# 320 free bytes in front of the activation tiles of a one-core transformer kernel

## The reference: what is computed

```python
def swiglu(h, w_gu, w_down):
    gate, up = jnp.split(h @ w_gu, 2, axis=-1)
    return (jax.nn.silu(gate) * up) @ w_down

for layer in range(2):
    x = x + 0.5 * swiglu(rmsnorm(x, ffn1_norm[layer]), ffn1_w_gu[layer], ffn1_w_down[layer])
    x = x + mixer(rmsnorm(x, mix_norm[layer]))
    x = x + 0.5 * swiglu(rmsnorm(x, ffn2_norm[layer]), ffn2_w_gu[layer], ffn2_w_down[layer])
x = rmsnorm(x, final_norm)
proj = rms_norm(x) @ w_in                      # second block
x = x + (gates0 * (attn @ w_up_attn) + gates1 * (rw @ w_up_rwkv)) @ w_out
x = x + jnp.square(jax.nn.relu(rms_norm(x) @ w_ff1)) @ w_ff2
x = x + (p @ w_ple) * jax.nn.sigmoid(rms_norm(x) @ w_ple_gate)
```

## The kernel before, in words

| tiles | place before |
|---|---|
| `w_hi`, `raw`, `w_lo` (all slots), `xT`; also `q_dec` and `att_t` of group 1, `gram_raw`, `x_raw`, `xt_raw` | 128 |
| `p_hi`, `p_lo` | 64 |
| `sq`, `rstd`, `full3` | 832 |
| `h_hi`, `h_lo`, `g_hi`, `g_lo`, `act2`, `full2`, `qkv`, `ao_*`, `mg_*`, `rw_*`, `gram` | 832 |
| `ba_hi`, `ba_lo`, `o_hi`, `o_lo`, `state_a`, `v_new`, `q_dec` and `att_t` of group 0 | 576 |
| `x_r`, `xt_r` | 64 |

## Time and profile before

### The profile page before, as it was taken

The page is one execution under the profiler, slowest core; times in us unless marked ns, Lnnn a source line. Parts: engine busy times, 40 slices in busy tenths (PEclk is TensorE's granted clock), DMA queues, the critical chain, the costliest instruction groups (busy, mean ns, idle before and its releaser), DMA issues. The chain is left out here.

```text
span 1605.0 us, 36127 instructions
## 1 busy us (share of the span) xinstructions
PE 1536.2 (96%) x15669; PEld 1478.2 (92%) x15669; DVE 1064.6 (66%) x1277; ACT 730.3 (46%) x814; POOL 69.9 (4%) x52
## 2 busy tenths in 40 slices
PE   7999989999999999999998999999997889999998
PEld 6999989878999999999988999999886778999997
DVE  5766487764867547664677766467768776777436
ACT  5443345543534344433446433354565444555333
POOL 2000000100100001000101000021000000100000
PEclk9999999999999999999999999999999999999999
DMA  8665545201556556555533555564320012555552
GB/s 269 189 192 201 185 157 169 96 2 51 183 188 193 200 184 184 183 184 187 181 131 96 182 187 191 185 201 145 120 79 3 3 56 81 184 184 189 202 186 79
DMA packets 155065, 243.26 MB, mean 152 GB/s; under 512 B 9283, under 2 KB 106174, under 8 KB 154814
## 3 DMA queue, kind: packets, MB, share of 16 engines
q1 hardware_dynamic: 154510, 240.63, 45.7%
q10 hardware_dynamic: 432, 0.79, 0.2%
HBM read 240.34 MB, written 1.05 MB: 150 GB/s over the span
## 5 line engine op out<-in xcount | busy, mean ns | idle before, releaser
L2888 DVE TENSOR_TENSOR w_lo<-raw,w_hi 128x2048 fp32r<-128x2048 f32 x225 | 522.9, 2335 | 243.0 <-ACT w_hi L2715 242.1
L2518 PE MATMUL dense_ps<-h_hi,w_hi 128*128 128x256 f32 x2368 | 668.3, 282 | 12.2 <-DVE h_lo L2963 8.6
L2519 PE MATMUL dense_ps<-h_lo,w_hi 128*128 128x256 f32 x2368 | 662.0, 280 | 0.0
L2520 PE MATMUL dense_ps<-h_hi,w_lo 128*128 128x256 f32 x2368 | 662.0, 280 | 0.0
L2715 ACT ACTIVATE w_hi<-raw 128x2048 fp32r<-128x2048 f32 x225 | 428.5, 1913 | 332.6 <-DMA raw<-in_ffn_w_down 116.2
L2518 PEld LDWEIGHTS dense_ps<-h_hi,w_hi 128*128 128x128 f32 x2368 | 450.5, 190 | 18.3 <-issue 17.8
L2519 PEld LDWEIGHTS dense_ps<-h_lo,w_hi 128*128 128x128 f32 x2368 | 447.4, 189 | 0.8 <-issue 0.5
L2520 PEld LDWEIGHTS dense_ps<-h_hi,w_lo 128*128 128x128 f32 x2368 | 448.1, 189 | 0.0
L2520 PE MATMUL dense_ps<-g_hi,w_lo 128*128 128x256 f32 x960 | 266.9, 278 | 0.0
L2518 PE MATMUL dense_ps<-g_hi,w_hi 128*128 128x256 f32 x960 | 266.9, 278 | 0.0
L2519 PE MATMUL dense_ps<-g_lo,w_hi 128*128 128x256 f32 x960 | 266.9, 278 | 0.0
(11 more groups left out here) (554 smaller groups left out, 1750.5 us busy)
## 6 DMA issues: line engine op xcount, KB each, us to landing
raw<-in_ffn_w_gu SPq DMA_DIRECT2D x176, 512.0 KB, 4.6
raw<-in_ffn_w_down SPq DMA_DIRECT2D x88, 512.0 KB, 4.1
raw<-in_w_ff SPq DMA_DIRECT2D x64, 512.0 KB, 4.2
raw<-in_w_in SPq DMA_DIRECT2D x36, 512.0 KB, 4.4
raw<-in_a_w_in SPq DMA_DIRECT2D x32, 512.0 KB, 4.3
raw<-in_a_w_out SPq DMA_DIRECT2D x8, 512.0 KB, 4.0
raw<-in_b_w_in SPq DMA_DIRECT2D x8, 512.0 KB, 4.2
raw<-in_b_w_out SPq DMA_DIRECT2D x8, 512.0 KB, 4.1
```

Of the source, the lines that this page charges most:

```text
L2518: pe.matmul(o, hi, mh, start=start, stop=False)
L2519: pe.matmul(o, hi, ml, start=False, stop=False)
L2520: return pe.matmul(o, lo, mh, start=False, stop=stop)
L2888: dve.tensor_tensor(w_lo[:, p % SLOTS, :], raw[:, p % SLOTS, :], w_hi[:, p % SLOTS, :].bitcast(F32), ALU.subtract).then_inc(lo_ready, 1)
```

## The change

Behind `full3` and in front of `h_hi` 320 bytes of each partition are left free. Everything that is placed from `h_at` or `arena` on moves up by 320 bytes; `y_tok`, which is placed from the end of the memory, stays. No instruction is added, removed or moved in order; only the addresses of the tiles change.

```diff
@@ -213,6 +213,7 @@
     sq = fixed.take("sq", [P, KD, T])
     rstd = fixed.take("rstd", [P, T])
     full3 = fixed.take("full3", [P, 3, 2, T])
+    fixed.at += 320
     h_at = fixed.at
     h_hi = fixed.take("h_hi", [P, KD, T], F32R)
     h_lo = fixed.take("h_lo", [P, KD, T], F32R)
```

## The result

The changed kernel takes **1652.36 us**, the median of four executions (1650.19 to 1656.09). The kernel before took 1603.21 us beside it (four executions, 1600.39 to 1608.98). The ratio is 1.0304, with a 95% interval of 1.0267 to 1.0341: slower by 3%, 49.2 us. The forecast was 1601.8 us with a range up to 1630, so it was wrong; the time is that of the rival "an even distance costs" (1650 us).

A forecast was written before the change was run, and what follows sets the result against it. The prediction took the pace of TensorE's large matmuls to bound the kernel. All terms were 0, leaving the profiled 1607.0 us, or 1601.8 us by the median of the other executions; range 1580 to 1630 us.

The forecast's parts named there:

- an even distance costs: Slower rival, large matmuls at L2518 to L2520: even distances in 64-byte units pace at 119.6 ns, 1650 us; chance 0.10.
- Instructions, queues, waits: 0.: Whole kernel: no instruction or wait added, removed or moved, every queue issues the same DMAs; cost 0.
- VectorE and ScalarE: 0, within 0.3 us.: Tiles moving from 832 to 128 keep their instruction times; only L618 might change, by 0.3 us either way; taken as 0.
- Addresses of the large matmuls: TensorE's 10,800 large matmuls: the moved operand leaves their pace alone; taken as 0, bounds -91.0 to +48.3 us.
- (a): L723 reads `q_dec` at distance 0 or 64 from `state_a`: 111.5 ns per step either way, so place does nothing.
- (b): Both paces occur at distance 192, and at 448 as well, so the present distance does not choose the pace.
- (c): Gate logits, distance 256, have a third pace, 119.6 ns, but also one place in PSUM and stationary tiles at 576.
- All at 119.6: +48.3 us: Bound for the large matmuls: 6,077 fast ones lose 6.4 ns each and 4,723 slow ones 2.0 ns.
- Faster: place decides which pace is stable.: Rival: an equal place puts every restart of the large matmuls into the fast pace, -20.8 us, 1581.0 us; chance 0.14.
- The farther form: Faster rival extended: large matmuls lose all excess over their columns, 106.7 ns each, 1511 us; below 113.2 ns chance 0.05.
- The sum that the prediction has by this figure: Large matmuls all at the skill's 109.2 ns, if place alone keeps the kernel from it: -67 us.
- One pace rules in all five feed-forwards: Sign that the forecast is wrong; if right, ffn0, ffn1, ffn4 stay fast and ffn2, ffn3 slow.

The follow-up runs named there:

- the 14 to 5 groups at 704: Kernel without the computation, 20 groups of 48 float32r matmuls behind growing waits at distance 704: 14 at 113.3 ns, 5 at 117.8.
- the sweeps: Kernels without the computation, only groups of float32r matmuls with the distance of moving operand from weights varied: 113.3 ns at 112, 120.0 at 0.
- the version at 128: Against the kernel before: `h` and `g` each cut from one tile, data 32 bytes in, distance 128 from the weights; 1641.25 us, ratio 1.0189.

## Why the prediction was wrong, point by point

**Instructions, queues, waits: 0.** Right. The counts are the same on every engine, and TensorE's longest waits in the hybrid stage are on the same lines with the same lengths (5.5 us behind `bk`, in both).

**VectorE and ScalarE: 0, within 0.3 us.** Right. The pair of the earlier trace rows after the change (group on VectorE by shape, 1220 to 1400 us):

```profile
L619 DVE COPY_PREDICATED xt_raw<-msk,gram_raw 128x128 f32<-128x128 uint8 x4 | 2.3, 568 | 0.0
L619 DVE COPY_PREDICATED xt_r<-msk,gram 128x128 f32<-128x128 uint8 x4 | 1.9, 484 | 0.0
```

`gram` came to 128, the place of `gram_raw`, and the difference of 84 ns (76 before) stayed, so the place of `gram` was never its cause. `xt_r` (384) still lies elsewhere than `xt_raw` (128), so its place is not cleared.

**"Addresses of the large matmuls ... I take 0, being nearest to (a)".** This is the step that failed: the term put at 0 measured 4.5 ns on each of the 10,800 matmuls, 49 us. Of the three rows I weighed, I chose one that could not speak. (a) are float32 matmuls, and they take 111.5 ns at the distances 0, 64, now 256, and in the run with 384 free bytes 192 (modulo 256): this form has no such effect at these places, while float32r has 120.0 ns at 0 and 113.3 or 117.8 at 64 and 192. I had written down the difference in type and passed over it. (b) "So the present distance does not choose the pace" was true, and the 14 to 5 groups at 704 confirm that a restart has a part in it. But it says only that this distance has two paces; that another has one of its own was left possible, and I read it as excluded. (c) was the right row: the only float32r matmuls of 256 columns at an even distance, with the only third pace. I discounted it for its one place in PSUM and its stationary tiles at 576. Both were innocent: the large matmuls have the same 120.0 ns without either, and the gate logits themselves have 113.3 ns once only their distance changes. Among three rows, the one with the same type and shape should have carried the term.

**The size of the rival.** "All at 119.6: +48.3 us" against a measured 49.2. The pace is 120.0 and not 119.6 (+4.3 us over 10,800; the 119.6 was 120.0 read from rounded starts), the mean of before 115.4 and not 115.1 (-3.2, in part because the counts of the earlier trace rows took in two or three matmuls too many, so that 113.3 and 117.8 came out as 113.2 and 117.6). That the two mis-sizes nearly cancel is luck. The rule named with it (in units of 64 bytes, even is slow and odd is not) held in every sweep of this form with the weights and the moving tiles each at one place: 118.6 ns or more at 0, 128, 256, 384 and 512, and 113.3 or 117.8 at the odd ones. Its place, L2518 to L2520, and its decision point, a pace above 115.1, were right as well. I gave it 0.10.

**Faster: place decides which pace is stable.** Not by this change, and not by an equal place, which gives 120.0 ns. But a place with one stable fast pace exists: at 112 all 43 groups of the sweeps and the feed-forwards read above are fast, and the kernel gains 15 us (the rival had 20.8). The farther form is refuted for this matmul: none of the 29 distances tried goes below 113.3 ns. The Trainium skill, "TensorE: Matmul & The Clock Gate", "Back-to-back issue gap", gives 109.2 ns for 256 columns as the gap of a matmul by itself, and other figures for pairs of load and matmul; bfloat16, in such pairs, has 109.2 ns in every group here, and float32r never less than 113.3. (The sum that the prediction has by this figure, -67 us, should be -64 us: 91.0 less 10,800 x 2.5 ns.) The same page's two independent read ports ("Step-by-step: what each phase is for"), by which no distance could matter, fit bfloat16 and the float32 rows, which show no effect of it; for float32r the measurement decides against them.

**What would show it.** "One pace rules in all five feed-forwards" came true, with 120.0 ns, which is 833 steps in 100 us. The weight loads went to 192 ns as I said they should, but the version at 128 shows that this was no test.

## What to carry to other kernels

Where TensorE's stream of float32r matmuls sets the time, read its pace from start to start and compare it with the columns at the granted clock; where it is above, or two stretches of the same code differ, move one operand by some bytes and measure, since 64 bytes in an address were worth 3% here and 112 instead of 192 gained 1.2% (weights at 128). A change of an allocation is therefore not free by itself: look at what it does to the distance between stationary and moving operand modulo 256. And a row of another data type is no evidence for a term, however near it lies otherwise.

## What was not expected of the hardware

- The pace of float32r matmuls of 256 columns depends on the distance between the two operands' addresses modulo 256: 120.0 ns at 0, 118.6 to 120.0 at 128, mostly 117.8 at 64, 113.3 or 117.8 at 192, 113.3 at 112. Steps of 4 bytes matter: 108, 112 and 116 have 120.0, 113.3 and 121.6. All this is at the full clock; at the half clock, 704 and 0 both have 213 ns.
- At one and the same distance two paces are stable for hundreds of matmuls, and a wait of half a microsecond can change the pace. Executions of the kernel before differ by up to 19 us, which fits that.
- With 512 columns the order is another (226.7 ns at 0, 233.4 at 192), and in bfloat16 and float32 nothing of it was seen at the places tried.
